# Output projection's first tile taken channel by channel as attention outputs come, its weights split earlier

## The reference, cut to what matters

```python
x = x + gate1 * (attention(q, k, v) @ w_o)          # layers 1 and 3: 16 heads of 64
o = rmsnorm(o, sub_g) * (1.0 - lambda_init)         # layer 2: 8 heads of 128, normed head by head
x = x + gate1 * (o.reshape(B, S, D_MODEL) @ w_o)    # w_o is 1024 x 1024
```

## Time and profile before

| | us |
|---|---|
| runs of the kernel before | 3215.5, 3215.21, 3213.24 (median 3215.21) |
| the profiled execution, its own time | 3212.77 |
| span in the profile | 3211.0 |
| PE busy | 3041.9 (95%) |
| DVE busy | 2082.0 (65%) |
| ACT busy | 1083.5 (34%) |
| POOL busy | 402.6 (13%) |
| granted TensorE clock, mean | 0.969 |

### The profile page before, as it was taken

How to read it: one execution, slowest core, us unless ns; L and a number is a source line. 1 busy time by engine, 2 the same in 40 slices (tenths; PEclk the granted TensorE clock), 3 DMA queues, 4 the chain that set the end, 5 groups by cost and what they waited for, 6 DMA issues and landing times.

```text
span 3211.0 us, 54161 instructions
## 1 busy us (share of the span) xinstructions
PE 3041.9 (95%) x21098; PEld 2779.3 (87%) x21098; DVE 2082.0 (65%) x4004; ACT 1083.5 (34%) x2250; POOL 402.6 (13%) x392
## 2 busy tenths in 40 slices
PE   8999999888999999998989899999999888999999
PEld 6899999776599999997865699999987668999999
DVE  7666666767756666667647566666667674766665
ACT  3222222326623222223335432222233563322221
POOL 3000000223310000002237310000012231000000
PEclk9999999989999999999989899999999899999999
DMA  8533323110023332331200213333231002222221
GB/s 340 204 118 119 129 91 131 47 56 1 23 96 132 118 126 96 118 110 40 81 29 7 81 62 136 118 131 118 98 108 53 4 1 79 79 79 65 68 76 47
DMA packets 47197, 290.11 MB, mean 90 GB/s; under 512 B 4945, under 2 KB 11345, under 8 KB 13265
## 3 DMA queue, kind: packets, MB, share of 16 engines
q1 hardware_dynamic: 47058, 288.21, 25.0%
HBM read 283.98 MB, written 4.21 MB: 90 GB/s over the span
## 4 chain that ended last, share of the span: by engine, by line
PE 87%; DVE 6%; ACT 2%; issue 1%; DMA 1%; POOL 1%; SPq 0%; POOLq 0%; DVEq 0%; ACTq 0%
PE psA L1960 39%; PE psB L1960 24%; PE psA L2062 3%; PE psA L2064 3%; PE psA L2063 3%; PE psB L1977 2%; PE psA L794 2%; PE psB L727 2%; PE psB L709 1%; PE psA L695 1%; PE psB L852 1%; POOL sq_sum L1913 1%; DVE top L1573 1%; DVE query L1529 1%; DMA m_stage<-w_mod_dram 1%
## 5 line engine op out<-in xcount | busy, mean ns | idle before, releaser
L1960 PE MATMUL psA<-h_hi,w_hi 128*128 128x320 f32 (+1 forms) x2848 | 654.3, 311 | 13.9 <-DVE h_lo L2441 13.9
L1960 PE MATMUL psA<-h_lo,w_hi 128*128 128x320 f32 (+1 forms) x2832 | 648.9, 310 | 0.0
L1960 PE MATMUL psA<-h_hi,w_lo 128*128 128x320 f32 x2816 | 644.6, 310 | 0.0
L2466 DVE SCALAR_TENSOR_TENSOR xT<-psB,mod,xT 128x128 f32<-128x128 f32 x752 | 379.0, 547 | 241.8 <-PE psB L1960 241.6
L1960 PEld LDWEIGHTS psA<-h_hi,w_hi 128*128 128x128 f32 x2848 | 477.9, 189 | 17.4 <-issue 15.7
L1960 PEld LDWEIGHTS psA<-h_lo,w_hi 128*128 128x128 f32 x2832 | 476.8, 189 | 0.0
L1960 PEld LDWEIGHTS psA<-h_hi,w_lo 128*128 128x128 f32 x2816 | 473.5, 189 | 0.0
L2520 DVE TENSOR_SCALAR conv<-u_raw,vec_sb 128x642 f32<-128x642 f32 x176 | 108.4, 616 | 444.5 <-ACT u_raw L2281 444.5
L2345 DVE TENSOR_TENSOR w_lo<-w_stage,w_hi 128x512 fp32r<-128x512 f32 x496 | 352.9, 758 | 27.8 <-ACT w_hi L2198 27.8
L1960 PE MATMUL psB<-g_hi,wo_hi 128*128 128x320 f32 x1280 | 299.3, 315 | 0.1
L1960 PE MATMUL psB<-g_hi,wo_lo 128*128 128x320 f32 x1280 | 295.3, 313 | 0.0
(11 more groups left out here) (261 smaller groups left out, 4805.4 us busy)
## 6 DMA issues: line engine op xcount, KB each, us to landing
w_stage<-weights_dram SPq DMA_DIRECT2D x124, 1024.0 KB, 5.1
m_stage<-w_mod_dram SPq DMA_DIRECT2D x96, 1024.0 KB, 8.3
wo_stage<-w_out_dram SPq DMA_DIRECT2D x44, 1024.0 KB, 4.8
yT_dram<-xT SPq DMA_DIRECT2D x8, 322.0 KB, 2.2
xT<-xT_dram SPq DMA_DIRECT2D x1, 1544.0 KB, 9.8
xT<-xT_dram SPq DMA_DIRECT2D x1, 1032.0 KB, 6.3
w_stage<-weights_dram SPq DMA_DIRECT2D x2, 512.0 KB, 17.8
rope_raw<-rope_dram SPq DMA_DIRECT2D x3, 256.0 KB, 2.5
```

Source lines behind the costliest of these rows:

```text
L1960: ins = pe.matmul(o, wp, xp[:, a:b], start=first and n == 0, stop=last and n == 2)
L2466: ins = dve.scalar_tensor_tensor(out=xT[:, d, c:c + w], in0=tokens(psB, slot)[i], scalar=gate[:, d, i:i + 1], in1=xT[:, d, c:c + w], op0=A ...
```

## The change

- `w_hi` units 0 to 3 of chunk cw are made by ACT inside the attention: in layers 1 and 3 in slot 71, right behind the last probabilities that ACT takes; in layer 2 in slots 43 and 44. ACT waits there for the last but one value product (`s_pv`), the last reader of `pt0` and `ptd0`.
- `w_lo` units 0 and 1 are made by DVE inside the attention: in slot 73 in layers 1 and 3; in layer 2 in slot 44, behind the copy of l7's output. The rest follows the attention as before.
- PE begins output tile 0 without waiting for all outputs: it waits for each channel tile k by itself (`ATT_READY`). In layers 1 and 3 tile 0 stands behind the attention's last instruction. In layer 2 it is spread over slots 45 to 48, k = 0, 1, then 2, 3, then 4 to 6, then 7, each behind what PE has otherwise in the slot, and it goes to `psA` in place of `psB`.
- SP's waits and loads are as before.

```diff
+        ATT_READY = {1: range(1, KT + 1), 2: [5, 5, 5, 5, 9, 9, 9, 10], 3: range(1, KT + 1)}
...
+        last = max(D_BC)
+        D_PROJ = {last - 2: range(0, 2), last - 1: range(2, 4), last: range(4, KT - 1), last + 1: range(KT - 1, KT)}
...
# attention_diff_pe, at the end of a slot
                 if s in D_PV:
                     pv(*D_PV[s])
+                if s in D_PROJ:
+                    proj_first(D_PROJ[s])
# attention_act, at the end of a slot
+                if s == len(UNITS_G) + 3:
+                    act.wait_ge(s_pv[l], KT - 1)
+                    split_first(range(4))
# attention_diff_act
+                if s in (max(D_COPY) - 1, max(D_COPY)):
+                    act.wait_ge(s_pv[l], DIFF_HEADS - 1)
+                    split_first((0, 1) if s == max(D_COPY) - 1 else (2, 3))
# attention_dve
+                if s == len(UNITS_G) + 5:
+                    lo_first((0, 1))
# attention_diff_dve
                 if s in D_COPY:
                     out_copy(D_COPY[s])
+                if s == max(D_COPY):
+                    lo_first((0, 1))
# PE
-            def proj_tiles(l, cg, dt, x):
-                for k in range(KT):
+            def proj_tiles(l, cg, dt, x, ks=range(KT), ready=None):
+                for k in ks:
+                    if ready is not None:
+                        pe.wait_ge(s_att[l], ready[k])
...
-                    (attention_diff_pe if l == 2 else attention_pe)(pe, l)
-                    pe.wait_ge(s_att[l], ATT_DONE[l])
-                    for dt in range(KT):
+                    def proj_first(ks):
+                        proj_tiles(l, cp, 0, (h_hi, h_lo, halves(psA if l == 2 else psB, 0)), ks, ATT_READY[l])
+                    if l == 2:
+                        attention_diff_pe(pe, l, proj_first)
+                    else:
+                        attention_pe(pe, l)
+                        proj_first(range(KT))
+                    for dt in range(1, KT):
                         if dt >= 2:
                             pe.wait_ge(s_mxadd[l], dt - 1)
...
# ACT, behind the attention
                     act.wait_ge(s_att[l], ATT_DONE[l])
-                    split_w(cw, range(UNITS))
+                    split_w(cw, range(4, UNITS))
# DVE, behind the attention
-                    for u in range(UNITS):
-                        lo_w(u, UNITS * cw + u + 1)
+                    lo_first(range(2, UNITS))
```

More of the change, by code:

```diff
@@ L762, in attention_pe, with attention_diff_pe @@
                     pv(*PV_PARTS[s])
-        def attention_diff_pe(pe, l):
+        def attention_diff_pe(pe, l, proj_first):
             kv = qkv[6]
@@ L874, in attention_diff_pe, with attention_act @@
                     pv(*D_PV[s])
-        def attention_act(act, own, l):
+                if s in D_PROJ:
+                    proj_first(D_PROJ[s])
+        def attention_act(act, own, l, split_first):
             kv = qkv[3]
@@ L972, in attention_act, with attention_diff_act @@
                     exp(s + 1)
-        def attention_diff_act(act, own, l):
+                if s == len(UNITS_G) + 3:
+                    act.wait_ge(s_pv[l], KT - 1)
+                    split_first(range(4))
+        def attention_diff_act(act, own, l, split_first):
             def exp(u):
@@ L1529, in lo_part, with attention_dve @@
             return dve.tensor_tensor(out, src, hi.bitcast(F32), ALU.subtract)
-        def attention_dve(dve, own, l):
+        def attention_dve(dve, own, l, lo_first):
             kv = qkv[3]
@@ L1655, in attention_dve, with attention_diff_dve @@
                     out_lo(PV_PARTS[s - 1][0])
-        def attention_diff_dve(dve, own, l):
+                if s == len(UNITS_G) + 5:
+                    lo_first((0, 1))
+        def attention_diff_dve(dve, own, l, lo_first):
             for i in range(2):
@@ L2043, in proj_tiles @@
                                   (x[0][:, k, :], x[1][:, k, :]), k == 0, k == KT - 1)
-                    if k == 3:
+                    if k in (3, KT - 1):
                         ins.then_inc(s_wused, 1)
-                ins.then_inc(s_wused, 1)
             for l in range(DEPTH):
@@ L2089, in _ @@
                                 ins.then_inc(s_wused, 1)
-                    (attention_diff_pe if l == 2 else attention_pe)(pe, l)
-                    pe.wait_ge(s_att[l], ATT_DONE[l])
-                    for dt in range(KT):
+                    cp = c0 + QKV_CHUNKS[l]
+                    def proj_first(ks):
[6 more added lines that the diff above has]
+                    for dt in range(1, KT):
                         if dt >= 2:
                             pe.wait_ge(s_mxadd[l], dt - 1)
-                        proj_tiles(l, c0 + QKV_CHUNKS[l] + dt // 4, dt,
-                                   (h_hi, h_lo, halves(psB, dt % 2)))
+                        proj_tiles(l, cp + dt // 4, dt, (h_hi, h_lo, halves(psB, dt % 2)))
                 norm_pe(2 * l + 1, (l, 0) if 1 <= l < DEPTH - 1 else None)
@@ L2262, in _ @@
                     act.wait_ge(s_qkv, l)
-                    (attention_diff_act if l == 2 else attention_act)(act, own, l)
                     cw = c0 + nq
+                    (attention_diff_act if l == 2 else attention_act)(act, own, l, lambda units: split_w(cw, units))
                     act.wait_ge(s_att[l], ATT_DONE[l])
-                    split_w(cw, range(UNITS))
+                    split_w(cw, range(4, UNITS))
                     for dt in range(KT):
@@ L2461, in norm_dve, with add_out @@
                             mod_raw_bias(11)
-            def add_out(slot, d, gate, done):
+            def add_out(slot, d, gate, done, ps=psB):
                 for i, (c, w) in enumerate(((CTX0, SEQ), (LAT0, DEC_SEQ))):
-                    ins = dve.scalar_tensor_tensor(out=xT[:, d, c:c + w], in0=tokens(psB, slot)[i],
+                    ins = dve.scalar_tensor_tensor(out=xT[:, d, c:c + w], in0=tokens(ps, slot)[i],
                                                    scalar=gate[:, d, i:i + 1], in1=xT[:, d, c:c + w],
@@ L2487, in _, with lo_first @@
                     qkv_dve(dve, own, lo_w, l)
-                    (attention_diff_dve if l == 2 else attention_dve)(dve, own, l)
                     cw = c0 + QKV_CHUNKS[l]
-                    for u in range(UNITS):
-                        lo_w(u, UNITS * cw + u + 1)
+                    def lo_first(units):
+                        for u in units:
+                            lo_w(u, UNITS * cw + u + 1)
+                    (attention_diff_dve if l == 2 else attention_dve)(dve, own, l, lo_first)
+                    lo_first(range(2, UNITS))
                     for dt in range(KT):
                         dve.wait_ge(s_wused, UNITS * (cw + dt // 4) + 2 * (dt % 4) + 2)
-                        add_out(dt % 2, dt, md[:, MOD_G1:MOD_G1 + KT, :], s_mxadd[l])
+                        add_out(dt % 2, dt, md[:, MOD_G1:MOD_G1 + KT, :], s_mxadd[l],
+                                psA if l == 2 and dt == 0 else psB)
                         for u in (2 * (dt % 4), 2 * (dt % 4) + 1):
```

## The result

The changed kernel takes 3193.41 us (median of 4 runs, 3192.59 to 3196.12) against 3215.36 for the kernel before (4 runs): a ratio of 0.9938, interval 0.9926 to 0.9949, so 21.95 us faster where 13.8 were forecast, and under the low end of the range. Its profiled execution took 3196.12 us, with a span of 3194.3, 16.7 less than the span before. Over all runs shown here the means are 3213.6 (42 runs of the kernel before beside the others) and 3194.4 (9 runs of the changed one), 19.2 us apart.

The account below looks back on a forecast made before the run. PE, busy 95% of the span, bounds the kernel, so gains come only where it idles or runs at half clock. 4.6 + 4.6 + 4.6 = 13.8 us off 3212.8 gives 3199.0, plus 2.4 for the median: 3201.4, range 3197.5 to 3207.0.

Parts of the forecast that it names:

- Layers 1 and 3: Attention's end to tile 0: 4.6 us gained in each layer, 2.9 from PE's gap and 1.7 from the clock.
- channel 7 and tile 1: Layers 1 and 3, next edges: h_lo and w_lo units 2 and 3 come in time, so PE waits for nothing.
- Layer 2, the attention's end: Products of tile 0 fit between the attention's steps, the broadcast runs at full clock; last output at 1824.0.
- The rival of the tile in the attention's way: Layer 2: tile 0's products delay the sums and last broadcast; total gain 9.8 to 11.5 us, about 3204.6; chance 0.12.
- Layer 2, the projection: DVE's order behind DMA holds tiles 2 and 3, stalls 0.9 and 3.1 us; gain 4.6, bounds 4.6 and 6.3.
- tile 3 starts at 1843.5: Layer 2's projection: tile 3 starts then instead of 1849.8, after PE idles 3.1 us; gain 6.3 us there.
- The landing: Layer 2: the first half of chunk cw+1 arrives 13.1 us after issue, moving only -0.4 with the attention's end.
- the 1.7 for it: Layer 2's projection: us taken off the 6.3 for a clock fall behind PE's 3.1 us gap.
- The 2.0 us and 436 GB/s: Layer 2's loads: quoted DMA rule by which 5 MB land at about 1838.5, making tile 3's gain 8.6 us.
- From tile 3 on every stage is PE's own and as before: After layer 2's tile 3: later stages are unchanged, so the whole 13.8 us reaches the end.
- Slower, by the clock: Rival, later stages: earlier start adds half-clock stretches at 1.7 us each, ten give 3218; chance 0.03.
- a free layer 2: Rival: DVE's loop doesn't cap layer 2, the half chunk lands much earlier; 10.4 us there, 3195.6 total; chance 0.05.

Follow-up runs that it names:

- after_again: The changed kernel run again, unedited, for a second profile: 3195.52 us, ratio 0.9941 to the kernel before.
- only2: The changed kernel with layers 1 and 3 put back as before, so only layer 2 is changed: 3205.97 us, ratio 0.9979 to the kernel before.
- wait13: The changed kernel, but in layers 1 and 3 PE waits for all outputs before tile 0, weights still split early: 3196.04 us.
- late: The changed kernel, but in layer 2 SP issues the first half of chunk cw+1 only after all eight w_lo units of cw: 3196.94 us.
- dve: The changed kernel, but in layer 2 DVE adds tile 0 before w_lo units 4 to 7, and tile 1 before the next chunk's units: 3193.04 us.
- before_again: The kernel before run once more, unedited, for a second profile: 3214.27 us, ratio 1.0003.
- only13: The changed kernel with layer 2 put back as before, so only layers 1 and 3 are changed: 3202.5 us, ratio 0.9966 to the kernel before.
- early2: The changed kernel, but in layer 2 tile 0 stands behind the whole attention and waits for all outputs, weights still early: 3201.04 us.

## Why the prediction was right, and where it was wrong

**Layers 1 and 3: right.** 4.6 each were forecast and 4.4 measured. The gap went, the clock stayed up, channel 7 and tile 1 waited for nothing. Tile 0 took 7.34 us in place of 7.14, which is the 0.2 that is missing.

**Layer 2, the attention's end: right.** The order of the steps, the broadcast at full clock and the 24 products ahead of it, which delay nothing, came as worked out. The rival of the tile in the attention's way is out: the broadcast's end to the copy of l7 is 1818.13 - 1811.36 = 6.8 us, where before it was 1822.25 - 1815.02 = 7.2.

**Layer 2, the projection: right in its mechanism, wrong in its size.** The step that failed is "tile 3 starts at 1843.5", with an idle of 3.1 us and a fall of the clock behind it: 4.6 us forecast, 7.5 to 7.7 measured. Two terms were mis-sized. The landing was taken as the kernel before had it, 16.4 us behind the attention's end, and is 15.0 in every kernel with tile 0 in the attention and the loads in their order (six profiles: changed, after_again, only2, wait13, late, dve) and 16.3 to 16.5 in every one without (four: before, before_again, only13, early2). And the idle that was left, 1.3 us in the record (1.6 by the prediction's count), doesn't bring the clock down, so the 1.7 for it was not due: 1.4 + 1.7 = 3.1. The prediction had taken the lower bound of its term because it forecast a gap of 3.1 us; the 1.4 us of wait13 and the 1.3 here passed at full clock, so the error in the landing brought the other with it. Why the landing differs stays open (see the last section). The 2.0 us and 436 GB/s that the prediction quotes from the Trainium skill, DMA: Bandwidth & Descriptors, in Anatomy of one DMA, stand there for transfers that GpSimd issues, and these loads are SP's; the forecast doesn't use them.

**"From tile 3 on every stage is PE's own and as before": wrong.** FFN 1 gained 1.45 us and qkv 2 some 0.7, in the nine profiles with layer 1 changed and in none of the three without, but for wait13, whose FFN 1 gained 0.9 and whose qkv 2 nothing. For FFN 1 the trace shows the way. After the last tile PE does the norm's small work, and the clock falls. In the kernel before it fell while PE was at the norm's first wait and came back 4.5 us after PE's restart at 949.91:

```profile
940.50:941.00 0.50, 0.00 (x0) 0.80 0.00 0
...
954.00:954.50 0.50, 0.50 (x3) 0.54 0.00 0
954.50:955.00 0.50, 0.50 (x6) 1.00 0.00 0
```

In the changed kernel it fell 5.2 us after the last tile's last product (934.79) in place of 4.0 (936.78), so that the norm's products ran at full clock, and came back 3.0 us after the restart at 947.24:

```profile
940.00:940.50 0.50, 0.50 (x5) 0.52 0.77 197
...
950.00:950.50 0.50, 0.50 (x4) 0.74 0.00 0
950.50:951.00 0.50, 0.50 (x5) 1.00 0.00 0
```

1.5 us less of half clock behind the restart is 0.75, and the restart itself came 0.7 earlier (8.9 us in place of 9.6 behind the norm's last addition of squares): 1.45 together. The stretch at half clock is 13.7 us long in the three profiles with layer 1 as before and 10.2 in the nine others. In qkv 2 the clock stood at 0.50 for 13.7 us in the same three (182.4 to 182.8 for the stage), for 10.2 in eight (181.8 to 182.0) and for 17.1 in wait13 (183.1), so the 0.7 us go with the clock too. The rival *Slower, by the clock* had this mechanism and expected harm from it; it was a gain. It repeats in every profile, so it isn't chance of single runs, but I had no way to tell its sign beforehand.

**The sum.** 13.8 + 3.1 (layer 2) - 0.4 (layers 1 and 3) + 2.1 (FFN 1 and qkv 2) = 18.6 us. The means of all runs differ by 19.2. The 21.95 of the first four runs hold about 3 us more, which are put down to the spread of the runs: the first stage alone moves by 4 between executions, with 24 us at half clock in its shortest (dve) and 34 in its longest (only2). That part is luck; without it, by the 3194.4 of the means, the time still lies under the range.

**The range** was too narrow on its lower side. It left 10.4 us for a free layer 2 at a chance of 0.05, and gave the later stages 1 to 2 us of play.

## What to carry to other kernels

Where an engine stands empty before a product whose inputs mostly exist, there are two things to take off the path, the late inputs and the one wait for all of them, and what each is worth must be read at its place. Of layer 2's 7.5 us the early weights gave 1.0 and tile 0 taken by channels 6.5; of the 4.4 us in layers 1 and 3 the early weights gave 3.0 and the channels 1.4. Then look at the next edge in the order of the engine that drains the results: here DVE's loop put additions behind a subtraction that waited for a DMA, and took 2.8 us of the 10.3. A stage that nothing was changed in can still move by a microsecond or two through the granted clock; a range should have room for that on both sides, and the stages' lengths over several profiles show it where medians don't.

## What the runs showed of the hardware that I had not expected

The clock's falls and returns repeat in some stages and not in others. At FFN 1's norm each kernel has its own stretch at half clock in every profile, although the executions start differently by up to 4 us. At FFN 3's norm one and the same kernel has two lengths, 13.7 us in its first profile (2711.53 to 2725.19) and 17.1 in its second (2709.46 to 2726.53), and FFN 3 is 1.5 us longer in the second. Windows of PE, of the first and then of the second profile:

```profile
2711.50:2712.00 0.50, 0.00 (x0) 0.53 0.00 0
2725.00:2725.50 0.50, 0.50 (x5) 0.81 0.00 0
```

```profile
2709.00:2709.50 0.50, 0.00 (x0) 0.96 0.00 0
2726.50:2727.00 0.50, 0.50 (x5) 0.97 0.00 0
```

The Trainium skill, TensorE: Matmul & The Clock Gate, in What's actually happening, has the observation behind the clock run free of the kernel. The two lengths at FFN 3 and the moved fall in before_again fit that. The repeat at FFN 1 alone doesn't speak against it, and no run here shows why it repeats.

The landing in layer 2 differs by 1.4 us with the same 4 MB ahead and at any time of issue. One thing goes with it in the ten profiles with SP's loads in their order: an instruction fetch of 16 KB on the queue q8. In the six with tile 0 inside the attention it starts 1.1 to 1.8 us ahead of the attention's end (DMA queues of the stretch 1816.31 to 1820.31, changed kernel: packets, MB, share of the 16 engines):

```profile
q8 instruction: 1, 0.02, 1.6%
```

In the four others it starts 7.6 to 8.9 us behind that end, in the busy stretch of the loads, as in the kernel before (1832.42 to 1836.42):

```profile
q1 hardware_dynamic: 233, 1.67, 99.8%
q8 instruction: 1, 0.02, 1.4%
```

1.4% of 16 engines for 4 us is 0.9 us of one engine. That the fetch makes the 1.4 us is argued from this coincidence and not shown; no run moved the fetch alone. In layer 1 it falls among the loads in both kernels (8.2 and 4.3 us behind the attention's end), and the landing is the same there (13.5 us).
